# A 27-phase fp32 kernel: five weight slots and three high slots, compression tiles inside the projection, an earlier table load

## What is computed

```python
# first block
mem_kv = rms_norm(mem, g_mem) @ w_mem_kv          # first phases, "mk" and "mv"
...
x = x + rms_norm(mixed @ w_out, g_post_mix)        # ends with phase "wo"
h2 = rms_norm(x, g_pre_ffn)
y2 = (silu(f_gate) * f_up) @ w_ffn_out             # ends with phase "fo1"
x = x + rms_norm(y2, g_post_ffn)
# second block
out = s5_mixer(...)                                # ends with phase "so"
x = x + gate * out
kv = h_kv @ w_kv                                   # phase "kvt" (16 weight units), then "kvn"
kc = gelu(flat(blocks of kv[0]) @ w1 + b1) @ w2 + b2   # compression, w1 are the 4 "cw" units
vc = the same for kv[1]
```

## Time and profile before

| what | value |
|---|---|
| median of 3 runs | 3064.54 us (3064.34 to 3067.28) |
| the profiled execution | 3066.89 us, span 3065.1 us |
| TensorE busy | 3016.8 us, 98% of the span |
| VectorE busy | 2205.7 us, 72% |
| ScalarE busy | 1483.0 us, 48% |
| mean granted TensorE clock | 0.995 |
| loads of ring halves | 1272, median 4.6 us from issue to landing |

### The profile page before, as it was taken

One profiled execution on the slowest core, in us unless ns is written; L12 is line 12 of the kernel. 1 busy time (PEld: TensorE's weight loads), 2 busy tenths in 40 slices (PEclk: granted clock), 3 DMA queues, 4 the chain that ended last, 5 costly groups with the idle time before them and its releaser, 6 DMA issues.

```text
span 3065.1 us, 46429 instructions
## 1 busy us (share of the span) xinstructions
PE 3016.8 (98%) x16676; PEld 2553.0 (83%) x16676; DVE 2205.7 (72%) x2677; ACT 1483.0 (48%) x2001; POOL 358.6 (12%) x397
## 2 busy tenths in 40 slices
PE   8999999999999999999999999899999999999998
PEld 8888888888888888888888888799888888888887
DVE  6779887667767766886766765899875657566665
ACT  6455444454444345444444443656554544555553
POOL 0000000025555431550000000000000000000000
PEclk9999999999999999999999999999999999999999
DMA  7667776658888876998888985555555578544445
GB/s 249 217 234 282 248 277 220 197 185 310 306 282 315 309 268 183 302 301 254 287 285 256 267 278 192 159 200 197 179 189 185 181 274 309 197 153 151 151 165 192
DMA packets 272833, 719.25 MB, mean 235 GB/s; under 512 B 27456, under 2 KB 120128, under 8 KB 271360
## 3 DMA queue, kind: packets, MB, share of 16 engines
q1 hardware_dynamic: 251616, 669.28, 65.2%
q10 hardware_dynamic: 13936, 28.69, 2.9%
q0 software_dynamic: 7088, 18.62, 1.7%
HBM read 699.96 MB, written 16.53 MB: 234 GB/s over the span
## 4 chain that ended last, share of the span: by engine, by line
PE 90%; DVE 4%; DMA 2%; ACT 2%; issue 1%; ACTq 0%; SPq 0%; DVEq 0%
PE psum L881 60%; PE psum L818 11%; PE psum L862 6%; PE psum L821 5%; DMA ring<-in_stream 2%; DVE ring_parts L2527 1%; PE psum L920 1%; PE psum L933 1%; PE psum L999 1%; PE psum L1138 1%; ACT hi_parts L1496 1%; PE psum L1289 1%; PE psum L841 0%; PE psum L1007 0%; PE psum L947 0%
## 5 line engine op out<-in xcount | busy, mean ns | idle before, releaser
L2527 DVE TENSOR_TENSOR ring_parts<-ring,hi_parts 128x1024 fp32r<-128x1024 f32 x1000 | 1220.2, 1251 | 404.8 <-ACT hi_parts L1496 399.6
L1496 ACT ACTIVATE hi_parts<-ring 128x1024 fp32r<-128x1024 f32 x1000 | 1025.3, 1057 | 769.5 <-DMA ring<-in_stream 740.7
L881 PE MATMUL psum<-hi_parts,arena_low_parts 128*128 128x512 f32 x3440 | 1100.9, 391 | 4.3 <-DVE ring_parts L2527 4.2
L881 PEld LDWEIGHTS psum<-hi_parts,arena_low_parts 128*128 128x128 f32 x3440 | 645.9, 188 | 142.9 <-issue 5.3
L881 PE MATMUL psum<-hi_parts,arena_high_parts 128*128 128x512 f32 x2224 | 731.4, 394 | 1.1 <-DVE arena_high_parts L2252 1.1
L881 PE MATMUL psum<-ring_parts,arena_low_parts 128*128 128x512 f32 x1872 | 728.9, 389 | 0.0
L881 PEld LDWEIGHTS psum<-hi_parts,arena_high_parts 128*128 128x128 f32 x2224 | 418.1, 188 | 90.5 <-issue 3.9
L881 PEld LDWEIGHTS psum<-ring_parts,arena_low_parts 128*128 128x128 f32 x1872 | 351.7, 188 | 71.3
L881 PE MATMUL psum<-ring_parts,arena_high_parts 128*128 128x512 f32 x960 | 374.1, 390 | 0.0
L818 PE MATMUL psum<-arena_low_parts,hi_parts 128*128 128x512 f32 x992 | 321.0, 399 | 2.7 <-DVE ring_parts L2527 2.7
L862 PE MATMUL psum<-arena_low_parts,hi_parts 128*128 128x256 f32 (+1 forms) x1184 | 232.4, 287 | 2.1 <-DVE ring_parts L2527 1.4
(11 more groups left out here) (418 smaller groups left out, 2682.9 us busy)
## 6 DMA issues: line engine op xcount, KB each, us to landing
ring<-in_stream SPq DMA_DIRECT2D x1272, 512.0 KB, 4.6
ssm_kept<-work POOLq DMA_DIRECT2D x16, 512.0 KB, 6.8
arena_high<-ssm_kept ACTq DMA_DIRECT2D x11, 512.0 KB, 4.4
frac_kept<-work POOLq DMA_DIRECT2D x15, 256.0 KB, 6.0
early<-frac_kept ACTq DMA_DIRECT2D x15, 256.0 KB, 2.7
work<-ssm_kept ACTq DMA_DIRECT2D x5, 512.0 KB, 4.4
arena_high<-in_mem ACTq DMA_DIRECT2D x8, 256.0 KB, 7.1
arena_high<-in_x ACTq DMA_DIRECT2D x1, 2048.0 KB, 13.0
```

The source lines that it names most:

```text
L881: mm = pe.matmul(stream_bank(b + t), r32(x[part][:, kg * KG + kk, t * P:(t + 1) * P]), r32(cols), start=(kg == 0 and kk == 0 and n == 0), ...
L1496: act.activation(r32(hi[:, g % RING, cols]), ring[:, g % RING, cols], ACT.Copy).then_inc(hi_made, 1)
L2527: dve.tensor_tensor(r32(slot), slot, as32(hi[:, g % RING, cols]), ALU.subtract).then_inc(cut_done, 1)
```

## The change

Five weight slots and three high slots take the place of four and four (the same memory). A high slot is indexed by the count of cut units instead of by the plan entry, and its ScalarE cut waits for the release of the unit three cut units earlier (`SPLIT`). The `cw` entries 0 and 1 move behind `kvt` unit 9, entries 2 and 3 behind unit 13, and the two `cmp_hidden` steps with them. At the start, the second part of `cst` on SyncE goes behind the first ring half, ScalarE runs a one-element copy ahead of its first cut, ScalarE's wait for `cst` comes behind that cut, and the loads of the tables and of `early` move from the beginning to just ahead of that of `x`.

```diff
-RING, UNIT = 4, 2048
+RING, HI_RING, UNIT = 5, 3, 2048
...
+    if _name == "kvt":
+        _cw = [("unit", "cw", _u) for _u in range(4)]
+        _list = _list[:10] + _cw[:2] + _list[10:14] + _cw[2:] + _list[14:]
+    elif _name == "cw":
+        _list = []
...
-    s = [("norm", "x3", j) for j in range(KT // 2)] + spread("kvt")
-    s += [("cmp_hidden", 0), ("cmp_hidden", 1)]
+    s = [("norm", "x3", j) for j in range(KT // 2)]
+    s += between(spread("kvt"), {9: [("cmp_hidden", 0)], 13: [("cmp_hidden", 1)]})
...
+SPLIT = [_g for _g, _x in enumerate(PLAN) if _x[0] == "unit" and _x[1] != "cw"]
...
-        hi = two_types("hi", [P, RING, UNIT])
+        hi = two_types("hi", [P, HI_RING, UNIT])
...
+        def slot_of(w, g):
+            return w[:, (HI[g] - 1) % HI_RING if w is hi else g % RING, :]
...
             sp.dma_start(cst[:, 0:128], A["cst"][:, 0:128]).then_inc(consts_landed, 16)
-            sp.dma_start(cst[:, 896:CST], A["cst"][:, 896:CST]).then_inc(consts_landed, 16)
...
                 sp.dma_start(halves_of_ring[:, s, :], A["stream"][s]).then_inc(landed[s], 16)
+                if s == 0:
+                    sp.dma_start(cst[:, 896:CST], A["cst"][:, 896:CST]).then_inc(consts_landed, 16)
...
-            act.dma_start(cst[:, 128:896], A["cst"][:, 128:896]).then_inc(tables_landed, 16)
-            act.dma_start(early[:, 0:512], A["early"]).then_inc(tables_landed, 16)
...
-                    if g >= RING:
-                        value = 2 * (g - RING) + h + 1
+                    if HI[g] > HI_RING:
+                        value = 2 * SPLIT[HI[g] - 1 - HI_RING] + h + 1
                         act.wait_ge(units_done, value if i is None else i * (2 * per) + value)
...
             act.wait_ge(consts_made, CONSTS_MADE)
+            did(act.activation(stat[:, 45:46], ones[:, 0:1], ACT.Copy))
+            cut(0, halves_=(0,))
             act.wait_ge(consts_landed, 32)
-            cut(0, halves_=(0,))
             steps(MIXER[:KT // 4])
+            act.dma_start(cst[:, 128:896], A["cst"][:, 128:896]).then_inc(tables_landed, 16)
+            act.dma_start(early[:, 0:512], A["early"]).then_inc(tables_landed, 16)
             act.dma_start(x_in, A["x"].rearrange("(t p) n -> p t n", p=P)).then_inc(x_landed, 16)
```

More of the change, by code:

```diff
@@ L132, in segment @@
     for x in PLAN[POS[("unit", phase, 0)]:]:
-        if x[0] == "unit" and x[1] != phase:
+        if x[0] == "unit" and x[1] not in (phase, "cw"):
             break
-        out += [x]
+        out += [x] if x[1] != "cw" else []
     return out
@@ L705, in _ @@
         def _(sp):
+            halves_of_ring = ring[:].rearrange("p s (h n) -> p (s h) n", h=2)
             sp.dma_start(cst[:, 0:128], A["cst"][:, 0:128]).then_inc(consts_landed, 16)
[L707 to L708 removed]
             for s in range(2 * RING):
@@ L817, in wide_unit @@
                         if form == "wide":
-                            mm = pe.matmul(bank, r32(hi[:, slot, cols]), both_parts(x, kk), start=(kk == first_ks[0]),
+                            mm = pe.matmul(bank, r32(slot_of(hi, slot)[:, cols]), both_parts(x, kk), start=(kk == first_ks[0]),
                                            stop=(kk == KT - 1))
                         else:
-                            mm = pe.matmul(bank[:, 0:S], r32(ring[:, slot, cols]), r32(x[0][:, kk, :]), start=False, stop=False)
+                            mm = pe.matmul(bank[:, 0:S], r32(slot_of(ring, slot)[:, cols]), r32(x[0][:, kk, :]), start=False, stop=False)
                     if all(j // (KT // 2) != h for j in first_ks[n + 1:]):
@@ L840, in first_wide_pair @@
                             for n, (w, moving, bank) in enumerate(order):
-                                mm = pe.matmul(bank, r32(w[:, slots[u], cols]), moving, start=(k == 0 and n == 0),
+                                mm = pe.matmul(bank, r32(slot_of(w, slots[u])[:, cols]), moving, start=(k == 0 and n == 0),
                                                stop=(k == KT - 1 and n == 1))
@@ L861, in t_unit @@
                         for n, (w, part) in enumerate(((hi, 0), (hi, 1), (ring, 0))):
-                            mm = pe.matmul(bank[0:m, half:half + S], r32(w[:, slot, cols]), r32(x[part][:, k, :]),
+                            mm = pe.matmul(bank[0:m, half:half + S], r32(slot_of(w, slot)[:, cols]), r32(x[part][:, k, :]),
                                            start=(k == 0 and n == 0), stop=(k == KT - 1 and n == 2))
@@ L920, in last_pair @@
                                     mm = pe.matmul(stream_bank(b + t), r32(x[part][:, kg * KG + kk, t * P:(t + 1) * P]),
-                                                   r32(w[:, slot, cols]), start=False,
+                                                   r32(slot_of(w, slot)[:, cols]), start=False,
                                                    stop=(kg == groups - 1 and kk == KG - 1 and n == 2))
@@ L1495, in cut @@
                     cols = slice(h * HALF, (h + 1) * HALF)
-                    act.activation(r32(hi[:, g % RING, cols]), ring[:, g % RING, cols], ACT.Copy).then_inc(hi_made, 1)
+                    act.activation(r32(slot_of(hi, g)[:, cols]), ring[:, g % RING, cols], ACT.Copy).then_inc(hi_made, 1)
             def square(phase, c, t):
@@ L2526, in cut @@
                             continue
-                        dve.tensor_tensor(r32(slot), slot, as32(hi[:, g % RING, cols]), ALU.subtract).then_inc(cut_done, 1)
+                        dve.tensor_tensor(r32(slot), slot, as32(slot_of(hi, g)[:, cols]), ALU.subtract).then_inc(cut_done, 1)
                         continue
```

10 lines of the change are left out of this document (5 added, 5 removed).

## The result

| | median | lowest to highest | executions |
|---|---|---|---|
| before | 3064.81 us | 3062.13 to 3068.03 | 11 |
| changed | 3073.54 us | 3071.10 to 3076.89 | 11 |

The ratio is 1.0029, with a 95% interval of 1.0021 to 1.0037: the change makes the kernel 8.7 us slower, 6.4 to 11.3 us by the interval. The prediction was 3072.3 us, or +7.8. The profiled execution took 3073.54 us, with a span of 3071.8 us. (That of the kernel before stands some 2 us above its own median, so the two spans lie closer together, 6.7 us, than the medians.)

The account below looks back on a forecast made before the run. TensorE was taken as the bound, busy 3016.8 of 3065.1 us, so only its idle stretches count. 11.3 - 3.7 + 0 + 0.2 = +7.8 us on the median 3064.54 gave 3072.3 us, range 3064.5 to 3077.

Parts of the forecast that it names:

- Ends of phases (1c): Ends of `wo`, `fo1`, `so`: three high slots delay cuts and tile 0's work; 2.2 + 4.7 + 4.4 = 11.3 us lost.
- I take nothing: Clock behind the new 2.2 us wait at the end of `wo`: no extra cost, at most 2 us more.
- The ring (1a): Waits for cut weight halves at L881 and L818: five slots start loads earlier, gaining 3.7 us; bounds 2 and 6.5.
- mostly vanish: Sign in the changed profile: ScalarE's waits for `ring` landings would mostly disappear.
- Regular flow (1b): Units away from phase ends: ScalarE's cut waits for an earlier unit's release, covered by 8.6 us a unit; cost nothing.
- Compression tiles (2): `cmp_hidden` steps within `kvt`: cuts of units 10 and 14 stay covered by 1.0 us; cost 0, bounds -1 and +1.
- The start (3): Kernel start: copy takes 1.28 us table load off the first cut, later DMA issues eat it; +0.2 us, bounds -1.3, +1.2.
- (a): Ends of phases not held up, since the engines find the high slot free; 3061.0 us, no measurable change; chance 0.08.
- (b): TensorE's pace over 500 cut units improves by 0.025 us each, winning 12.5 us; 3059.8 us; chance 0.04.
- (c): Held-up ends are real, but ring and start win their upper bounds: +2.5 us, 3067.0; chance 0.22 for 3066 to 3070.6.
- (d): Slower clock in `wo`, weak ring, start and compression tiles at upper cost: +13.5 us, 3078.0; chance 0.1 for above 3076.

Follow-up runs that it names:

- the treated kernel: Kernel before with five ring and three high slots, the cuts at the ends of `wo`, `fo1` and `so` made later; 3059.31 us against 3064.93, ratio 0.9982.

## Why the prediction was right

**Ends of phases (1c).** The mechanism is shown: going to three high slots alone brings it, and moving the cuts behind tile 0's work takes it away, with all slots unchanged. The prices were 2.2 + 4.7 + 4.4 = 11.3; in the profile of the changed kernel they are 2.8 + 4.6 + 4.2 = 11.6, and by the medians the three cost 12.0. In `fo1` the wait was foretold as 11.6 us, 4.7 more than 6.9. It is 5.43 + 6.61 = 12.0, on two rows, since a small preparing matmul (L1284) stands between; but the kernel before had 0.8 us on the first of these rows too, which the prediction left out, so the two together grew by 4.4. In `so` 7.82 was foretold as near 8.0. In `wo` the transposes start 11.83 us behind the pair's start where they started 9.53 behind it, 2.3 us for the 2.2 foretold. There "I take nothing" for the clock was right in two of four profiles and missed 0.4 and 0.8 us in the two others, all behind the same wait of 2.14 us. That is inside the bound of 2, but the reason given (2.2 us is nearer to 1.27 than to 3.60) does not decide it.

**The ring (1a).** Predicted -3.7, measured -3.6 and -5.3. The waits that were counted are gone. That the size fits is in part luck. The sum rests on the one profile of the kernel before, with 4.2 us of waits at L881; the seven profiles with four ring slots have 1.8 to 4.9 us there, 3.0 in the mean, against 1.3 in all with five. So on average only 1.7 us of these waits go, and the rest of the measured gain, as far as it is real, must come from elsewhere; the last section has what is known. ScalarE's waits for landings did not "mostly vanish" either: 407 of 740.7 us are left.

**Regular flow (1b).** The 182 us for which ScalarE now waits for a release cost TensorE nothing that shows: with the ends treated, four ring and three high slots stand at -0.3 us, uncertain by 2.8.

**Compression tiles (2).** Nothing, as predicted, within 2.8 us. The first `cmp_hidden` runs from 2451.11 for 3.94 us, ScalarE's four cut halves from 2451.70 lie beside it, and TensorE has no wait for a cut half in `kvt`.

**The start (3).** Here the sum was mis-sized: +0.2 predicted, +1.7 measured alone (bound +1.2), uncertain by 2.8 us. The single steps came true or better: TensorE at 8.52 (9.3 foretold), the second cut at 16.44 (17.1). The second is right by two errors that cancel: the issues took 16.44 - 12.21 = 4.23 us instead of 3.65, but began at 12.21 instead of near 13.5. And the sum followed the wrong half. It ended at unit 0, but what counts is the second half of unit 2, two units later: in all twelve profiles beside that of the kernel before, `s5_rows` is late against it by what this cut is late, to within 0.15 us (2.5, 1.8 and 2.1 us in the three kernels with the whole new start, 0.9 or less in all others). In these three ScalarE waits 2.2 to 2.5 us for the half's landing, elsewhere at most 0.7. The prediction had costed nothing for what the later issues do to the ring's own landings.

So the whole start costs about 2 us there. It is not the late start of TensorE, which comes as late (8.7) in the kernel with the tables loaded early, and not the moved tables alone, nor the copy with the earlier cut alone. It takes the late tables together with something of the rest. With what, and by which queue, stays open; the moved part of `cst` was never tried alone.

The copy's table load was 1.28 us and the copy followed at once, at 6.43; the rule of the Trainium skill ("ScalarE: Activation LUTs", section "What ACT_TABLE_LOAD costs") that adds a drain of 1.38 us has no row here either.

**The rivals.** (a), ends not held up, is out: the waits are there. (b), 12.5 us from TensorE's pace, is out too: its busy time is 3016.8 us in both profiles, though over all kernels there may be 1 to 2 us of it (below). (c) needed a ring of 6.5 us and a start that wins, and the start loses. (d) fails on the sum: the slower clock in `wo` came, but cost about 0.5 us and not 2, and the ring was not weak.

## What to carry over

When a ring of buffers is made shorter, ask not only how far ahead the regular flow runs, but who holds a buffer longest: here a pair that keeps its halves until a second pass. Then look at what stands behind the refill in program order on each engine: the refill could wait (in the treated kernel VectorE cut half 1 of `su` 1 at 1956.17, 30 us after the pair's start, and TensorE never waited for it), the work behind it could not. The cure here was to move the refill, not to give the slot back: that turned +6.3 us into -5.6. And read each wait from several profiles before it goes into a sum: the 4.2 us of waits that the fifth slot was to remove were in part the draw of one execution.

## What the runs showed of the hardware

**The clock behind a short wait.** The same wait in the same place costs clock in one execution and not in the next. Behind the 2.14 us at the end of `wo` the granted clock fell to 0.50 in two profiles and stayed at 1.00 in two. A wait of 1.53 us (at 2959.81, L1007) in the kernel before was followed by 0.50, the same wait of 1.54 us (at 2968.11, L1018) in the changed kernel by 1.00 (one window of each; the granted clock is again the third value from the end):

```profile
2962.00:2964.00 2.00, 2.00 (x10) 1.90 (x9) 1.83 (x6) 0.00 (x0) 0.00 (x0) 0.50 0.00 0
```

```profile
2970.00:2972.00 2.00, 2.00 (x14) 1.80 (x14) 1.83 (x7) 0.00 (x0) 0.00 (x0) 1.00 0.00 0
```

A wait of 1.84 us (at 2197.32 in the kernel before, 2202.46 in the changed one) was followed by 0.50 in both, and the 1.27 us in the earlier trace rows by 1.00. So what such a wait costs in clock can't be read from one profile, and a sum should give it as a range.

**TensorE's pace.** Single profiles of this kernel differ by more than the parts of the change. From the start of `ff0` to the last pair of `fo1` the profiles with five ring slots took 725.5 to 726.3 us (six kernels), those with four 726.9 to 731.4 (seven, the kernel before with 729.4). The means, 725.9 and 728.6, are 2.7 us apart. In this stretch TensorE never waited for a cut half with five slots and 1.4 us in the mean with four. The other 1.2 us are busy time: 725.4 to 726.3 us with five slots and 726.4 to 727.8 with four, for the same matmuls. The two groups just miss each other, so a small gain in pace from the fifth slot is likely, but no experiment isolates it and its cause stays open. Over the whole span the groups overlap (3012.7 to 3018.6 us for the 16676 matmuls, with a mean of 3014.3 with five slots and of 3016.6 with four).

The four-slot kernel with the ends treated shows how far a single execution can mislead: the profiled one took 3060.44 us, the median of its eleven is 3065.42. A shift of 2 to 4 us in one profile is not evidence; the medians, or the same landmark in several kernels, are. What sets the pace from execution to execution stays open.
